# First mixer of a two-mixer decoder step: decayed keys by block transposes and a round trip through HBM, block sums at another place, last head and last pair in another order

## What is computed

```python
# mixer A (HGRN2), 8 heads of 128: per head and chunk
q, f, v, gate = split(rms_norm(x) @ w_in)          # D_MODEL -> 4 x 1024
logf = log(lb + (1 - lb) * sigmoid(f));  k = (1 - lb) * sigmoid(-f)
cum = cumsum(logf)                                  # in a chunk
o = (q * exp(cum)) @ S + sum_{s<=t} (q_t . k_s exp(cum_t - cum_s)) v_s
S = exp(cum_last) * S + (k * exp(cum_last - cum)).T @ v     # decayed keys x values
x = x + (rms_norm(o) * silu(gate)) @ w_o
# then keys, values, forget gates once, for mixer B
# mixer B (forgetting attention), 16 heads of 64, causal softmax with a cumulative
# log-forget bias; the samples attend to 8 pages of 128 cached rows each
x = x + (attention * silu(gate)) @ w_o_b
```

## Time and profile before

| | |
|---|---|
| runs | 1508.12, 1508.76, 1510.18 us, median 1508.76 |
| profiled execution | 1508.85 us, its span 1507.1 us |
| mean granted TensorE clock | 0.999 |
| PE busy | 1473.0 us (98%) |
| DVE busy | 1000.5 us (66%) |
| ACT busy | 670.8 us (45%) |
| GpSimd (POOL) busy | 416.5 us (28%) |
| DMA | 308.96 MB, mean 205 GB/s |

### The profile page before, as it was taken

How to read it: one execution, slowest core, us unless ns; L and a number is a source line. 1 busy time by engine, 2 the same in 40 slices (tenths; PEclk the granted TensorE clock), 3 DMA queues, 4 the chain that set the end, 5 groups by cost and what they waited for, 6 DMA issues and landing times.

```text
span 1507.1 us, 24074 instructions
## 1 busy us (share of the span) xinstructions
PE 1473.0 (98%) x8757; PEld 1083.9 (72%) x8757; DVE 1000.5 (66%) x1995; ACT 670.8 (45%) x1364; POOL 416.5 (28%) x335
## 2 busy tenths in 40 slices
PE   7999999999999999999999999999999999998998
PEld 6788888888888875445777777777777777764443
DVE  5878696978878684126467676768767667757321
ACT  4434545444444552212265555645555555545100
POOL 6012322121212100012051535344342625432200
PEclk9999999999999999999999999999999999999999
DMA  9985757767675734423236869696877879598731
GB/s 267 277 237 158 226 166 210 224 203 228 184 229 159 226 139 129 119 65 129 61 116 188 272 182 308 193 276 203 274 252 224 275 216 306 178 339 318 262 125 58
DMA packets 296267, 308.96 MB, mean 205 GB/s; under 512 B 26502, under 2 KB 252030, under 8 KB 296150
## 3 DMA queue, kind: packets, MB, share of 16 engines
q1 hardware_dynamic: 285014, 270.84, 58.9%
q0 software_dynamic: 11136, 36.59, 7.2%
HBM read 247.76 MB, written 126.73 MB: 248 GB/s over the span
## 4 chain that ended last, share of the span: by engine, by line
PE 86%; DVE 6%; ACT 4%; issue 2%; DMA 1%; POOL 0%; SPq 0%; DVEq 0%; POOLq 0%; ACTq 0%
PE psum L2179 44%; PE psum L2203 7%; PE psum L2692 7%; PE psum L2490 5%; PE psum L2516 4%; PE psum L2256 3%; PE psum L2142 2%; PE psum L2450 2%; PE psum L2548 2%; ACT psum L1307 1%; PE psum L2322 1%; PE psum L2267 1%; ACT psum L1316 1%; PE psum L2338 1%; PE psum L2342 1%
## 5 line engine op out<-in xcount | busy, mean ns | idle before, releaser
L2179 PE MATMUL psum<-arena 128*128 128x252 f32 (+1 forms) x3472 | 812.4, 385 | 2.4 <-DVE arena L1484 2.2
L2179 PEld LDWEIGHTS psum<-arena 128*128 128x128 f32 x3472 | 642.2, 190 | 124.4 <-issue 24.3
L985 POOL TENSOR_TENSOR arena<-arena 128x1024 f32<-128x1024 f32 x64 | 157.0, 2453 | 376.4 <-DMA arena<-k_pages 370.5
L1484 DVE TENSOR_TENSOR arena<-arena,psum 128x252 f32<-128x252 f32 (+1 forms) x310 | 129.2, 417 | 153.3 <-PE psum L2179 148.5
L2692 PE MATMUL psum<-arena 128*128 128x512 f32 x256 | 113.9, 598 | 1.6 <-DVE arena L1906 1.6
L2203 PE MATMUL psum<-arena 128*128 128x512 f32 x256 | 113.0, 595 | 0.1
L1060 ACT COPY arena<-psum 128x252 f32<-128x252 f32 (+1 forms) x124 | 46.2, 373 | 139.9 <-PE psum L2179 139.8
L2692 PEld LDWEIGHTS psum<-arena 128*128 128x128 f32 x256 | 47.2, 190 | 59.3 <-issue 56.9
L2203 PEld LDWEIGHTS psum<-arena 128*128 128x128 f32 x256 | 47.6, 191 | 57.3 <-issue 56.4
L1123 ACT ACTIVATE arena<-arena 128x1024 f32<-128x1024 f32 x48 | 50.6, 1055 | 85.4 <-DVE arena L1530 84.9
L1307 ACT ACTIVATE psum<-psum,arena 128x640 f32<-128x640 f32 (+3 forms) x64 | 58.9, 921 | 60.7 <-DVE arena L1839 60.7
(11 more groups left out here) (270 smaller groups left out, 2050.8 us busy)
## 6 DMA issues: line engine op xcount, KB each, us to landing
k_pages<-in_cache_k SPq DMA_DIRECT2D x64, 512.0 KB, 6.6
v_pages<-in_cache_v SPq DMA_DIRECT2D x64, 512.0 KB, 7.1
arena<-k_pages SPq DMA_DIRECT2D x64, 512.0 KB, 5.2
arena<-v_pages SPq DMA_DIRECT2D x64, 512.0 KB, 6.8
arena<-in_w_in_a SPq DMA_DIRECT2D x32, 512.0 KB, 7.1
arena<-in_x_prompt SPq DMA_DIRECT2D x16, 512.0 KB, 7.8
arena<-in_w_kv SPq DMA_DIRECT2D x16, 512.0 KB, 6.5
arena<-in_w_in_b SPq DMA_DIRECT2D x16, 512.0 KB, 7.5
```

Source lines behind the costliest of these rows:

```text
L985: pool.tensor_tensor(k_ring[:, m % 2], k_ring[:, m % 2], q_all[:, m % S:m % S + 1, :].broadcast_to([P, PAGES, P]), ALU.mult).then_inc(kq_m ...
L1484: dve.tensor_tensor(out, more, bank[n % 2][:, 0:size(u)], ALU.add).then_inc(of.by_dve, 1)
L2179: ins = pe.matmul(bank[n % 2][:, 0:size(u)], w[:, k, :], x[:, k, :], start=(k == 0 and r in (0, 1, 3, 4)), stop=(k == HK - 1), skip_group_ ...
```

## The change

1. `k_dec` now lies in `t1`. `exp_kd` is made on ACT between level 8 and level 4; `k_dec` on DVE behind `merge(4)`. DVE turns it with a second `turn_tokens` into `k_blocks` (area `o_rs`), SP stores and reloads it (`TOKEN_SETS = 2`), in ordinary heads behind the values' load. The transposes on PE and the copies on ACT are gone. The update is 32 products of 32 columns and stands behind `fq(8, 9)`; on DVE `fq(8)` stands before `chunk_states(0)`, and `o_row` before the gate step.
2. GpSimd makes the F, Q sums of head h + 2 at the end of head h (from `fq(10)` on, the last of the four steps after `fq(12)`).
3. Last head: DVE turns the values behind `factors(2)`; SP sends both stores and both loads before `w_o`'s second half and `res_in`.
4. Last pair: on DVE `gate_in` behind `shift`, `y_add(0, 1)` before `smp_out`; on PE one y matmul group more before `scores(4)` and one less behind it.

```diff
 PT_AT = (0, 0, 0)
-TOKEN_SETS = 1
+TOKEN_SETS = 2
 MOVES = 16
...
         k_h, q_h, sg_h, logf, cum, q_dec = area(N), area(N), area(N), area(N), area(T), area(T)
-        k_dec = logf[:, 0:T]
+        k_dec = t1[:, 0:T]
...
         o_rs = area(N)
-        k_dec_tok = o_rs[:, 0:T].rearrange("p (t k) -> p t k", k=P)
+        k_blocks = o_rs[:, 0:T]
+        k_dec_tok = k_blocks.rearrange("p (g t l) -> p t g l", g=4, l=32)
         s_all = area(NC * P).rearrange("p (c v) -> p c v", v=P)
...
         smp_done = Marks(sem("smp_done"), "k_smp", "v_smp", "o_row", "o_smp", "mean_smp")
-        uu_done = Marks(sem("uu_done"), "outer0", "outer1", "turn0", "turn1", "upd0", "upd1")
+        uu_done = Marks(sem("uu_done"), "outer0", "outer1", "upd0", "upd1")
         ob_done = Marks(sem("ob_done"), "o0", "o1")
...
         lv_taken_v, lv_taken_a = sem("lv_taken_v"), sem("lv_taken_a")
-        uu_taken_v, uu_taken_a = sem("uu_taken_v"), sem("uu_taken_a")
-
-
-        acts = Marks(sem("acts"), "ln_f", "ln_q", "sig_q", "exp64", "k", "decays", "exp32", "exp_cum", "exp16", "exp8", "exp4", "exp2",
-                     "s_kept", "exp1", "exp_kd", "ln_g", "sq_smp", "ln_smp", "sig_g")
+        uu_taken_v = sem("uu_taken_v")
+
+
+        acts = Marks(sem("acts"), "ln_f", "ln_q", "sig_q", "exp64", "k", "decays", "exp32", "exp_cum", "exp16", "exp8", "exp_kd", "exp4", "exp2",
+                     "s_kept", "exp1", "ln_g", "sq_smp", "ln_smp", "sig_g")
         vecs = Marks(sem("vecs"), "logf", "cum", "q_in", "diff64", "k_in", "q", "fact64", "diff32",
                      "fact32", "diff16", "fact16", "diff8", "k_smp", "fact8", "diff4", "fact4", "diff2", "v_diag", "fact2", 
-                     "fact1", "k_dec", "g_in", "o_row", "o_smp", "q_dec", "sg")
+                     "k_dec", "fact1", "o_row", "g_in", "o_smp", "q_dec", "sg")
         o_strips_set, o_strips_stored, o_rs_loaded = sem("o_strips_set"), sem("o_strips_stored"), sem("o_rs_loaded")
...
             def tokens_in(h, n, blocks):
-                sp.wait_ge(rows_stored, STORES * token_set(h, n))
+                sp.wait_ge(rows_stored, STORES * token_set(h, TOKEN_SETS - 1 if h == AH - 1 else n))
                 sp.dma_start(blocks, token_rows[n]).then_inc(pt_moved, 16)
...
                         sp.dma_start(o_heads[n], o_dram[n]).then_inc(o_loaded, 16)
+                    tokens_out(h, 0, v_blocks)
+                if h < AH - 1:
+                    tokens_in(h, 0, v_blocks)
+                    tokens_out(h, 1, k_blocks)
+                else:
+                    tokens_out(h, 1, k_blocks)
+                    tokens_in(h, 0, v_blocks)
+                tokens_in(h, 1, k_blocks)
+                if h + 1 == AH:
                     sp.dma_start(w_o[:, AH // 2:AH], w_o_rows[:, AH // 2:AH]).then_inc(w_o_loaded, 16)
...
                     res_in(1)
-                    tokens_out(h, 0, v_blocks)
-                tokens_in(h, 0, v_blocks)
-                if h < AH - 1:
+                else:
                     sort_pages(sp, h + 1, 1)
...
-            def block_sums(one, two, out, done):
+            def block_sums(one, two, out, done, last_free=None):
...
                 me.chain(pool.tensor_tensor(out[:, 1], out[:, 0], one[:, 0:HK], ALU.subtract))
+                if last_free:
+                    pool.wait_ge(*last_free)
                 pool.tensor_tensor(out[:, 2], one[:, HK:KT], out[:, 1], ALU.subtract).then_inc(done, 1)
-            def w_sums(h, y1, y2, out, done):
+            def w_sums(h, y1, y2, out, done, last_free=None):
                 par = h % 2
                 pool.wait_ge(w_a_loaded[par], w_a_in(h))
-                block_sums(w_a[:, par, :, y1, :], w_a[:, par, :, y2, :], out, done)
+                block_sums(w_a[:, par, :, y1, :], w_a[:, par, :, y2, :], out, done, last_free)
...
                 pool.dma_start(s_smp, state_in[h]).then_inc(state_loaded, 16)
-                if h + 1 < AH:
-                    if h:
-                        pool.wait_ge(units.done, fq_unit(h, 14))
-                    w_sums(h + 1, F, Q, sums_fq, fq_sums)
+                if h == 0:
+                    w_sums(1, F, Q, sums_fq, fq_sums)
                 if 0 < h < AH - 1:
...
                 pool.dma_start(prompt_out[h], s_all[:, NC - 1, :]).then_inc(prompt_stored, 16)
+                if h + 2 < AH:
+                    pool.wait_ge(units.done, fq_unit(h + 1, 11))
+                    w_sums(h + 2, F, Q, sums_fq, fq_sums, last_free=(units.done, fq_unit(h + 1, 13)))
...
                 level(8)
+                for t in range(NC):
+                    end = t * P if t >= NC // 2 else t * P + C - 1
+                    ins = act.activation(t1[:, cols(t)], cum[:, cols(t)], ACT.Exp, bias=cum[:, end:end + 1], scale=-1.0)
+                ins.then_inc(acts.sem, 1)
                 level(4)
...
                 fq(2)
-                for t in range(NC):
-                    end = t * P if t >= NC // 2 else t * P + C - 1
-                    ins = act.activation(t1[:, cols(t)], cum[:, cols(t)], ACT.Exp, bias=cum[:, end:end + 1], scale=-1.0)
-                ins.then_inc(acts.sem, 1)
                 act.wait_ge(*units.taken(vg_unit(h, 13)))
...
                 act.activation(sg_h, sg_h, ACT.Ln, bias=1.0).then_inc(acts.sem, 1)
-                for j in range(2):
-                    act.wait_ge(uu_done.sem, uu_done.at(f"turn{j}", h))
-                    act.copy(k_dec_tok[:, 4 * j:4 * j + 4, :], bank[4 + j][:, :]).then_inc(uu_taken_a, 1)
                 v("o_smp")
...
                 vg(13)
-                dve.wait_ge(*units.taken(vg_unit(h, 9)))
-                dve.wait_ge(*units.taken(vg_unit(h, 12)))
-                turn_tokens(0, v_blocks, raw_v[:, 0:T])
+                if h + 1 < AH:
+                    dve.wait_ge(*units.taken(vg_unit(h, 9)))
+                    dve.wait_ge(*units.taken(vg_unit(h, 12)))
+                    turn_tokens(0, v_blocks, raw_v[:, 0:T])
                 dve.wait_ge(smp_done.sem, smp_done.at("v_smp", h))
...
                 fq(1)
+                if h + 1 == AH:
+                    dve.wait_ge(*units.taken(vg_unit(h, 9)))
+                    dve.wait_ge(*units.taken(vg_unit(h, 12)))
+                    turn_tokens(0, v_blocks, raw_v[:, 0:T])
                 merge(4)
+                a("exp_kd")
+                dve.tensor_tensor(k_dec, k_h[:, 0:T], t1[:, 0:T], ALU.mult).then_inc(vecs.sem, 1)
+                dve.wait_ge(vecs.sem, vecs.at("k_dec", h))
+                turn_tokens(1, k_blocks, k_dec)
                 a("s_kept")
...
                 fq(4)
-                a("exp_kd")
-                dve.tensor_tensor(k_dec, k_h[:, 0:T], t1[:, 0:T], ALU.mult).then_inc(vecs.sem, 1)
                 merge(1)
                 fq(5)
+                dve.wait_ge(smp_done.sem, smp_done.at("o_row", h))
+                dve.tensor_copy(o_row, bank[6][:, 0:2 * P]).then_inc(vecs.sem, 1)
                 a("ln_g")
...
                                          op1=ALU.subtract).then_inc(vecs.sem, 1)
-                dve.wait_ge(smp_done.sem, smp_done.at("o_row", h))
-                dve.tensor_copy(o_row, bank[6][:, 0:2 * P]).then_inc(vecs.sem, 1)
                 fq(6)
...
                 dve.wait_ge(s_all_free, h + 1)
+                fq(8)
                 chunk_states(0)
-                fq(8)
                 chunk_states(1)
...
                 row_max(p, 4)
-                gate_in(p)
+                if nxt:
+                    gate_in(p)
                 fin(p, 1)
...
                     shift(p - 1, 1)
+                if not nxt:
+                    gate_in(p)
                 turn_blocks(p, 4, 0, 1)
...
                 row_max(p, 6)
+                last(0, 1)
                 if p:
...
                 vg(1)
-                last(0, 1)
                 score(m + 3)
...
                 fq(5)
-                v("k_dec")
-                for j in range(2):
-                    pe.wait_ge(uu_taken_v, 4 * h + 5 + j)
-                    for t in range(4 * j, 4 * j + 4):
-                        ins = pe.transpose(bank[4 + j][:, t % 4 * P:(t % 4 + 1) * P], k_dec[:, cols(t)], ident)
-                    ins.then_inc(uu_done.sem, 1)
                 for b in range(S):
...
                 fq(7)
-                pe.wait_ge(pt_moved, MOVES * token_set(h, 0))
-                pe.wait_ge(uu_taken_a, 2 * h + 2)
-                for j in range(2):
-                    for c in range(4 * j, 4 * j + 4):
-                        ins = pe.matmul(bank[4 + j][:, c % 4 * P:(c % 4 + 1) * P], k_dec_tok[:, block_of(c), :], v_tok[:, block_of(c)],
-                                        start=True, stop=True)
-                    ins.then_inc(uu_done.sem, 1)
                 pe.wait_ge(acts.sem, acts.at("sq_smp", h))
...
                   .then_inc(smp_done.sem, 1)
-                fq(8, 9, 10)
+                fq(8, 9)
+                pe.wait_ge(pt_moved, MOVES * token_set(h, 1))
+                for j in range(2):
```

(10 more changed lines are left out.)

## The result

The changed kernel takes 1528.53 us (median of 4 runs, 1527.59 to 1529.44) against 1509.47 us for the kernel before beside it: a ratio of 1.0125 (95% interval 1.0112 to 1.0137), 19 us slower. The forecast was 1516.5 us, with 1505 to 1525 as its range: the direction was right, the time lies outside. The profiled execution took 1528.53 us, with a span of 1526.7 us against 1507.1.

What follows compares the result with a forecast made beforehand. PE, busy 98% of the span, was taken to bound the kernel. Terms -5.5 + 1.5 - 0.5 + 0.3 + 11.2 + 2.0 - 1.3 = +7.7 us on a median of 1508.76 gave 1516.5 us, range 1505 to 1525.

Steps and rivals of the forecast that it cites:

- PE work: Seven ordinary heads: 64 transposes go (-0.89 us each), the narrower update products cost +0.10 each; -5.5 us.
- round trip: Ordinary heads: decayed keys stored and reloaded land at 375.5 to 377, PE needs them at 376.1; near tie, +1.5 us.
- `logf`: Head boundaries: one `logf` took 2.47 us beside the F, Q sums; sums made ahead leave it free, -0.5 us.
- F, Q sums against the gate product: Six heads: moved sums meet the gate product, which DVE starts first, so waits are rare; +0.3 us, bounds 0 and 6.
- last head: Last head of the first mixer: PE stands 11 us for `w_o` before `part(5)`; with smaller terms +11.2 us.
- clock: After the 11 us stand before `part(5)`, PE may run slow as after the opening's idle time; +2.0 us, ends 0 and 3.5.
- last pair: Last pair of the second mixer: `gate_in` move gains 0, `y_add(0)` going first gains; -1.3 us.
- before the outputs: Last head: `part(8)` no longer hides the state sums between update and outputs; +2.3 us.
- the outer product's wait: Last head: L2295's 1.60 us wait behind the values' turn falls to about 0.5; PE starts 1.1 us earlier.
- The rival of late trips: Rival: the decayed keys' round trip is late in every head, 7 x 1.5 us more, 1526 us; chance 0.15.
- the stand before L1906's products: Last pair: PE's 1.6 us wait for `y_add(0)` behind `smp_out` and `gate_smp` goes; -1.3 us.
- The wait before L2535: Last pair: `gate_in` behind `shift` removes this 2.2 us wait, but it moves to before L2490; 0 net.

Runs made afterwards that it cites:

- run 8: The kernel before with only the early block sums of F and Q added: 1510.42 us, ratio 1.0007.
- Run 5: The changed kernel with one wait more, so GpSimd's early F, Q sums start only after VectorE's gate product: 1520.98 us, ratio 1.0084.
- run 1: The changed kernel with only the second half of `w_o` issued ahead of the last head's token stores again: 1527.23 us, ratio 1.0116.
- Run 12: The kernel before, unchanged, run once for a second trace: 1509.51 us.
- run 3: The changed kernel with `gate_in` of the last pair put back ahead of `fin` and `shift`: 1530.49 us, ratio 1.0136.
- run 6: The changed kernel with `w_o`'s second half and both residual tiles ahead of the last head's token stores: 1519.72 us, ratio 1.0079.
- run 2: The changed kernel with GpSimd's F, Q block sums put back at the start of each head: 1525.3 us, ratio 1.0099.

## Why the prediction was wrong, step by step

| step | forecast, us | measured, us |
|---|---|---|
| PE work, round trip, `logf` in seven heads | -5.5 + 1.5 - 0.5 = -4.5 | 7 x (67.05 - 67.62) - 0.5 = -4.5 |
| F, Q sums against the gate product | +0.3, bounds 0 and 6 | 6 x 1.77 = +10.6 |
| last head and clock | +11.2 + 2.0 = +13.2 | 74.54 - 61.28 = +13.3 |
| last pair | -1.3 | 27.59 - 26.34 = +1.25 |
| opening, other | 0 | -1.3 + 0.3 |
| sum | +7.7 | +19.6 of span |

**The step that failed** is "They now meet the gate product ... DVE starts the gate product first, so a wait before `fq(13)` should be rare: +0.3 us, bounds 0 and 6". DVE does start before the sums, by 0.50 us, and that doesn't protect it: GpSimd was already issuing a DMA, the sums followed directly, and the product was held through two of them. Where it began 0.39 us into the first sum, with GpSimd idle before that, it cost 0.7 us (run 8). It isn't rare, it happens in all six heads that make such sums. And the upper bound came from the hold of `logf` in the one place that showed it, 1.2 us, without asking what two sums in a row do (2.8 us) and how little lies between the gate product and TensorE. Run 5 shows the step alone: the laps go back to 67.04 to 67.36 us, and its time of 1520.98 us lies inside the range; by the laps, with this term at nothing, the changed kernel would be at 1518.

**The last head** was right in its place, its cause and its size: `w_o` issued at 573.92 against 569.6 forecast, a stand of 10.03 against 11, a loss of 2.75 us to the clock against 2.0, 2.43 before the outputs against 2.3, the outer product's wait 0.47 against 0.5. What I didn't see is that `w_o` wasn't the only load behind the tokens: undoing that alone wins 1.3 us by the medians (run 1).

**The round trip** was right: a near tie. The weight loads of L2339 wait for `token_rows` 1.6 us in all, in four heads. The rival of late trips, which ends near the measured time, is wrong in its mechanism: run 5 leaves the trip alone and wins the laps back. (Its own sum, 1516.5 + 7 x 1.5, is 1527 and not 1526.)

**`logf`**, the -0.5: the operation is free as said (1624 to 1234 ns), but the half microsecond was one lap of 68.13 us in one execution. Run 12, the same kernel, has 67.62 us in this lap too. The opening's 1.3 us is of the same kind: in the changed kernel's trace the third group of its transposes starts at 18.73 us instead of 20.01 in code that the change doesn't touch, and in runs 1, 3 and 6 head 0's place, 115.61 here, is 114.84 to 116.24.

**The last pair**: the stand before L1906's products went from 1.57 to 0.21 as said. The wait before L2535 moved only in part: 1.54 of its 2.20 us are left, and 2.62 us before L2490 come on top. The term was lost in two places: the scores of row 5 start 1.0 us later, with a page that came 1.0 us later, and they and the products behind them run slow, 1.2 and 0.5 us, at a granted clock of 0.55 (1391.2 to 1394.0) where the kernel before had 1.00. Run 12 shows both in the kernel before, so they belong to the execution at least as much as to the order; how much is the order's stays open. One trace of before was too few for a term of this size.

**The clock.** Behind the stand for `w_o` the granted clock is 0.50, and the six products at 583.86 took twice their time. Behind the stand at the opening it is shown as 1.00, as in the kernel before, though the first eight transposes take 1.94 us again; that row stays unexplained. The Trainium skill (TensorE: Matmul & The Clock Gate, Part 1) says that an idle array goes back to 1.2 GHz until it has been busy again; this trace agrees at the stand for `w_o`.

## What to carry to other kernels

Where work is moved on GpSimd, find each operation of VectorE with two SBUF operands that runs near it, look at what GpSimd does at the moment this operation starts (a DMA issue counts), and price the meeting at the whole run of GpSimd operations behind each other, not at one; a single wait that keeps them apart can be worth all of it. Where a load is moved behind a store and its return on one queue, all loads behind it move too: restore one and the next one's wait appears. And a stretch that waits for a stream of pages differs by 2 us between two executions of one kernel, so terms of 1 us there need more than one trace.

## What the runs showed of the hardware

- A VectorE operation with two SBUF operands that had begun 0.50 us (gate product) or 0.15 us (`logf`) before two GpSimd additions of 1.27 us was held until both were done: 4.10 us for 1.29 and 3.75 for 1.23. GpSimd's third addition was then held by it: 2.15 us for 1.27. In both cases GpSimd was issuing a DMA when VectorE's operation started, and the additions followed with no gap.
- Where GpSimd was idle at that moment, VectorE kept its time and GpSimd was held, also in the changed kernel:
```profile
998.35 1.29 DVE L1820 SCALAR_TENSOR_TENSOR arena<-arena 128x1032 f32<-128x1032 f32 x1
998.46 3.38 POOL L996 TENSOR_TENSOR arena<-arena 128x1024 f32<-128x1024 f32 x1 [15.26 <-DMA arena<-k_pages]
```
  L996 takes 2.35 us alone. Counted over the 14 traces here (VectorE additions and products of over 0.3 us with two SBUF operands, and a GpSimd addition that starts while they run): in 205 meetings with GpSimd idle at VectorE's start, VectorE was held in none; in 36 meetings with GpSimd issuing a DMA at that moment, it was held in all. The DMA issue alone holds nothing (1.28 us in run 5). Why an issue in front turns the meeting round isn't shown, nor why `logf` in run 2 (GpSimd's addition 0.40 us ahead, 3.21 us) was held through two additions and the gate product in run 8 (0.39 us ahead, 1.97 us) through one; a run with a pause between the issue and the sums would be the next step.
- The Trainium skill (SBUF — State Buffer, SBUF: two separate sides) says that such an operation and a GpSimd operation that reads SBUF take a lock, and that whichever starts first has it for its whole instruction. The 205 meetings agree. The gate product agrees only if the DMA issue, 0.08 us ahead of it, counts as the one that was first; and that the later one is held through two instructions, and not one, is more than the page says.
- VectorE's additions with one operand in PSUM took 0.43 us beside GpSimd's additions, as without them (run 5).
- A 10.03 us stand of TensorE was followed by a granted clock of 0.50 and products of twice the length (5.49 us for 2.74). After a 1.50 us stand in head 4 the clock stayed at 1.00 (389.1 to 391.2) and eight products took 2.05 us, where eight take 1.95.
